# Eleven of the thirteen gate products that stand behind the RWKV chain move into seven earlier lumps

## What is computed

```python
def token_mixer(h, ...):
    p = h @ w_in
    p_r, p_m, p_g = jnp.split(p, [RWKV_COLS, RWKV_COLS + MLSTM_COLS], axis=-1)
    y_r = rwkv7_branch(p_r, ...) @ branch_w_rwkv
    y_m = mlstm_branch(p_m, ...) @ branch_w_mlstm
    g_r, g_m = jnp.split(jax.nn.sigmoid(p_g.astype(jnp.float32)), 2, axis=-1)
    return ((g_r * y_r + g_m * y_m) @ w_out).astype(h.dtype)
```

## Time and profile before

| what | value |
|---|---|
| median of 3 runs | 1408.33 us (1407.04 to 1410.0) |
| the profiled execution's own time | 1409.51 us |
| its span in the profile | 1407.5 us |
| PE busy | 1385.3 us, 98% of the span |
| granted PE clock, mean | 0.999 |
| share of PE in the chain that ended last | 96% |
| instructions on PE and PEld | 2 x 13536 |
| instruction packets on queue q8 | 106, 1.74 MB |

### The profile page before, as it was taken

One profiled execution on the slowest core, in us unless ns is written; L12 is line 12 of the kernel. 1 busy time (PEld: TensorE's weight loads), 2 busy tenths in 40 slices (PEclk: granted clock), 3 DMA queues, 4 the chain that ended last, 5 costly groups with the idle time before them and its releaser, 6 DMA issues.

```text
span 1407.5 us, 30467 instructions
## 1 busy us (share of the span) xinstructions
PE 1385.3 (98%) x13536; PEld 1304.2 (93%) x13536; DVE 1028.7 (73%) x1718; ACT 288.4 (20%) x556; POOL 67.6 (5%) x137
## 2 busy tenths in 40 slices
PE   7999999999999999999999999999999999999998
PEld 3999999888978999999999999988998889999998
DVE  5899889778524769897988886787873375856565
ACT  2211101452222031110031110034332302211101
POOL 5000000000000000100000000000000000000000
PEclk9999999999999999999999999999999999999999
DMA  9999785443423658888767886554433257456530
GB/s 347 325 328 326 284 316 172 141 141 106 113 71 122 236 183 269 278 303 291 246 211 254 275 280 237 167 133 151 140 90 96 65 192 251 144 188 209 195 136 30
DMA packets 214051, 283.10 MB, mean 201 GB/s; under 512 B 13289, under 2 KB 177505, under 8 KB 213921
## 3 DMA queue, kind: packets, MB, share of 16 engines
q1 hardware_dynamic: 194976, 211.11, 46.5%
q0 software_dynamic: 17952, 69.21, 14.0%
q10 hardware_dynamic: 992, 0.85, 0.2%
HBM read 280.10 MB, written 1.05 MB: 200 GB/s over the span
## 4 chain that ended last, share of the span: by engine, by line
PE 96%; DVE 2%; DMA 1%; issue 1%; ACT 0%; ACTq 0%; SPq 0%; DVEq 0%
PE ps L1833 94%; PE ps L1837 1%; DVE ada_acc L1045 1%; DMA ada_stage<-in_ada_w_dram 1%; DMA xn<-in_x_dram 0%; PE ps L2332 0%; DVE ada_turn L1051 0%; DVE ada_red L1052 0%; DVE arena L1274 0%; DVE arena L1277 0%; DVE arena L1275 0%; DVE hT L1818 0%; ACT xn L696 0%; ACT hT L696 0%; DVE x L1218 0%
## 5 line engine op out<-in xcount | busy, mean ns | idle before, releaser
L1833 PE MATMUL ps<-hT,ring 128*128 128x128 f32 (+2 forms) x2448 | 394.3, 318 | 3.4 <-issue 2.1
L1833 PEld LDWEIGHTS ps<-hT,ring 128*128 128x128 f32 (+1 forms) x2448 | 349.9, 190 | 37.7 <-issue 10.7
L1833 PE MATMUL ps<-y_both,arena 128*128 128x128 f32 x2304 | 266.6, 275 | 1.0 <-issue 1.0
L1833 PEld LDWEIGHTS ps<-y_both,arena 128*128 128x128 f32 x2304 | 261.8, 192 | 1.5 <-issue 1.5
L1833 PE MATMUL ps<-arena 32*32 32x32 f32 (+6 forms) x4368 | 203.1, 230 | 2.5 <-issue 2.4
L1833 PEld LDWEIGHTS ps<-arena 32*32 32x32 f32 (+3 forms) x4368 | 192.6, 138 | 11.9 <-issue 9.8
L1833 PE MATMUL ps<-arena,ring 128*128 128x128 f32 (+1 forms) x1312 | 186.5, 294 | 0.0
L1833 PEld LDWEIGHTS ps<-arena,ring 128*128 128x128 f32 x1312 | 171.3, 191 | 6.6
L1045 DVE SCALAR_TENSOR_TENSOR ada_acc<-ada_stage,cond,ada_acc 128x1024 f32<-128x1024 f32 (+1 forms) x119 | 149.0, 1252 | 5.6 <-DMA ada_stage<-in_ada_w_dram 1.6
L1833 PE MATMUL ps<-y_both,ring 128*128 128x128 f32 (+1 forms) x1024 | 150.8, 301 | 0.0
L1833 PEld LDWEIGHTS ps<-y_both,ring 128*128 128x128 f32 x1024 | 138.7, 192 | 6.5
(11 more groups left out here) (317 smaller groups left out, 1341.4 us busy)
## 6 DMA issues: line engine op xcount, KB each, us to landing
ring<-in_ffn_w_in_dram SPq DMA_DIRECT2D x86, 1024.0 KB, 7.7
ada_stage<-in_ada_w_dram POOLq DMA_DIRECT2D x66, 1024.0 KB, 5.7
ring<-in_ffn_w_out_dram SPq DMA_DIRECT2D x44, 1024.0 KB, 6.7
ring<-in_mix_w_in_dram SPq DMA_DIRECT2D x46, 512.0 KB, 5.2
ring<-in_mix_w_in_dram SPq DMA_DIRECT2D x12, 1024.0 KB, 5.7
ring<-in_mix_w_in_dram SPq DMA_DIRECT2D x6, 1536.0 KB, 6.4
ring<-in_mix_w_out_dram SPq DMA_DIRECT2D x8, 1024.0 KB, 5.0
arena<-in_ada_w_dram SPq DMA_DIRECT2D x6, 1024.0 KB, 13.6
```

Source lines behind the costliest of these rows:

```text
L1833: return nc.tensor.matmul(out_, lhsT, rhs, start=start, stop=stop, **kw)
```

## The change

Only the table of places changes. The sum of all places stays 96, the products keep their numbers, and so their order, their weights and their banks.

```diff
-GATE_PLACES = (("num", 5), ("n", 8), ("a", 8), ("b", 8), ("c", 8), ("d", 8), ("e", 8), ("f", 9), ("h", 7),
-               ("i", 4), ("j", 5), ("k", 5), ("tail", 13))
+GATE_PLACES = (("num", 5), ("n", 10), ("a", 10), ("b", 10), ("c", 9), ("d", 9), ("e", 10), ("f", 10), ("h", 7),
+               ("i", 4), ("j", 5), ("k", 5), ("tail", 2))
```

## The result

The changed kernel takes 1416.78 us (median of 6 runs, 1411.51 to 1419.99) against 1409.06 us of the kernel before on the same chip (6 runs, 1407.04 to 1410.07): 7.7 us or 0.5% slower, ratio 1.0049 with a 95% interval of 1.0032 to 1.0066. I had forecast 1408.8 us and a range that ended at 1412.0 us. Only the direction, slower, came as forecast; the size and the range were wrong. The 1416.8 us lies beyond even the slower rival (B).

A forecast was written before the change was run, and what follows sets the result against it. The prediction took PE's work plus the holes in it, late instruction packets, as the bound. Its terms, 0 + 0 + 0 + 0.5 us on a median of 1408.33 us, gave 1408.8 us, range 1404.4 to 1412.0 us.

The forecast's parts named there:

- rival (B): Tile 7's start in lump `i` puts the `branch_w_mlstm` transfer over 64x64-run packets in both layers: +4.1 us, 1412.4 us; chance 0.16.
- What bounds the kernel: Whole span: PE's work plus its holes, 6.1 us in both stretches, which are waits for the next instruction packet.
- the recipe for the size of the holes: Boundaries every 128 pairs; a packet needs 3.0 us quiet, 4.8 us inside a weight transfer, against PE's time on 128 pairs.
- Products that move: Eleven tail products, 4.75 us a layer, go into the lumps at the same size, bank and clock: net 0.
- What the lumps cover: In the lumps: no hole is ended by DVE or ACT, so longer lumps cover what is covered already: 0.
- What the tail covered: Behind the shorter tail: cover used up but not gone, some 0.9 us to spare at the transposes: 0.
- Rival (C): The tail's cover fails, `r normed` later than PE at the transposes: 1410.5 to 1411 us; chance 0.04.
- Instruction packets: Holes in both stretches: 4.4 us in layer 0 and 3.0 us in layer 1, recipe against recipe +0.5 us.
- The clock has nothing to give back.: Both stretches: PE's granted clock is already 1.00, the level of 2.4 GHz, so no gain was counted from it.
- The page's rule: Crossing a 256-instruction block is "mostly hidden"; by it the packet term would be 0 and the time 1408.3 us.

The follow-up runs named there:

- e2: The changed kernel with 36 small matmuls (72 pairs) more at PE's start, so all packet boundaries fall 72 pairs earlier: 1410.35 us.
- e3: The kernel before with 24 small matmuls (48 pairs) more at PE's start: 1413.93 us.
- e8: The kernel before with 46 small matmuls (92 pairs) more at PE's start, ahead of the wait for x: 1405.69 us.
- e7: The changed kernel with the SP wait of e1 and 76 pairs of small matmuls more at PE's start, ahead of the wait for x: 1401.80 us.
- e1: The changed kernel with SP waiting for 'chain 2' ahead of each layer's second `branch_w_mlstm` transfer, which also holds the `branch_w_rwkv` one behind it: 1408.56 us.
- e9: The changed kernel with SP holding back only each layer's first `branch_w_rwkv` transfer until 'chain 2': 1413.15 us.
- e11: e7 with the change undone: the places of before, SP's wait and the 76 pairs kept: 1404.26 us.
- e6: The kernel before with one forced hole a layer: PE waits for DVE's "r centred" ahead of the tail products: 1418.16 us.
- e4: The kernel before with the eleven tail products put into lump `h` alone, `n` to `f` as they were: 1415.57 us.

## Why the prediction was wrong

**What bounds the kernel** stood: PE's work and the holes in it, and the holes are instruction packets. e2, e3 and e8 move nothing but the boundaries, and so does e7 against e1; e1 and e9 move nothing but transfers. All shift the time by holes and clock, in the direction that this reading gives, though the recipe for the size of the holes missed in e3 and e11.

**Products that move, 0.** Right: no row of a gate product at full clock has another price per record, and e1 has the time of the kernel before.

**What the lumps cover, 0.** Right in that no hole is ended by DVE or ACT in either kernel.

**What the tail covered, 0.** Right, 0.93 us to spare where 0.9 was forecast. Rival (C) didn't come.

**Instruction packets, +0.5 us.** This step failed, in size: in the profiled execution the holes grew by 4.6 us (10.72 against 6.12 us). Layer 0 came as laid out: holes of 0.4, 1.4 and 2.5 us were forecast and 0.52, 1.69 and 2.17 us measured, at those places, and those of 1.13 and 1.34 us went. Layer 1 was forecast with 3.0 us and had 6.34 us. Of the 3.3 us missed, 2.1 us is the hole at the end of the run of 160 pairs, 3.56 us in place of 1.5. I had followed the `branch_w_mlstm` transfer through SP's queue and not the one queued behind it, which was then free to leave on its own at DVE's `qt`; e9 shows that one at work. Another 1.7 us is the hole ahead of lump `b`, 2.06 us in place of 0.4. Its packet met a transfer that SP had issued at 1069.23 us and started only as that burst ended, 13.3 us into the stretch. In e1 and e9, with the same order up to there, it started 12.9 and 12.3 us into the stretch, in e9 with q1 still at 115%, and the holes had 1.47 and 1.05 us: where in a burst the packet gets through varies between executions. That this packet meets a transfer at all may come from tile 3's start, two products earlier in `a`; no run tests that apart. Also wrong was to take 4.8 us as the most that a packet needs in traffic: from its boundary to 1134.95 us this one took nearly 6 us (2.43 us of records and 3.56 us of hole).

**"The clock has nothing to give back."** This sentence failed outright: it put the clock at 0 because it could not rise. But it could fall, and the forecast of a 2.5 us hole should have carried that price. The stretches of the kernel before have no hole that long, but its end has the sign: PE's last product is done at 1402.67 us, and the granted clock is 0.50 from about 1404.0 us on. Three falls of some 1.65 us are 5 us of the profiled execution's 10.5 us, as much as the holes. That execution is the slowest of the six, and over all of them the share is smaller: the mean granted clock of the six runs is 0.996, that of the 23 runs of the kernel before beside e1 0.9977. Over a span of 1418 us the difference is 2.4 us of the 7.7 us, an estimate, as each run's clock is given to 0.001 only. With the holes as I forecast them and one fall behind the 2.5 us, the term would have been +2.2 us and the time 1410.5 us; with the second transfer seen, a second fall and 2.1 us more, 1414.2 us.

**The rival (B)** had the mechanism and the place and was too cheap, for the same two reasons. It held "just not in layer 1, where lump `j` lies between", which is true of the first transfer only.

**The page's rule** (Trainium skill, "Runtime: NRT & Kernel Launch", section on instruction fetch mechanics), that the crossing of a block is mostly hidden: the runs agree in one place and not in another. Between the two stretches, 606.13 us with 4775 pairs and so some 37 crossings, all idle time of PE is 0.66 us. In the stretches the changed kernel pays 10.7 us of holes, and e7, with the same dense runs, none: there it depends on where the crossings fall and what transfers they meet.

What stays open: 1 us of e6, the 0.35 us in layer 0, why some holes of about 2 us are followed by a fall and others not, and how often exactly the timed runs have one. The changed kernel's runs spread over 8.5 us, and the profile shows only the slowest. The fastest, 1411.51 us, is the one with a mean granted clock of 0.999; the other five have 0.993 to 0.997. So it probably had no fall, and the 2.4 us that it still lost are holes.

## What to carry to other kernels

On an engine that runs many short instructions, lay the boundaries of its instruction packets over the program and look which weight transfer goes out at each: an edit that moves the release of a buffer moves that transfer and every one queued behind it, and a transfer over a dense stretch can stop the engine that it was meant to feed. Price a hole on PE not by its length alone: in these runs holes of 1.93 (e9), 2.06, 2.13, 2.17, 2.26, 2.27 and 3.56 us were followed by 3.4 us or more at half clock, while others of 1.95 (e1), 2.09 (e6) and 2.20 us (e4) were not. A kernel that differs by a few matmuls at its start is not the same kernel to the instruction queue, so a change of this size is judged only after the alignment has been varied too.

## What the runs showed of the hardware that I had not expected

The changed kernel took 1416.8 us, and 1401.8 us with 76 small pairs ahead of it and one wait on SP: 1% by the alignment and the time of two transfers, with every product kept. A packet of instructions can be held up by a weight transfer in progress: at all three long holes of the changed kernel it starts as q1 runs dry, while in the kernel before (386.1 us) and in e9 (1072.5 us) one got through with q1 at 107 and 115%. What decides this no run shows. And 38 small matmuls in four groups of rows took 1.28 us, inside PE's idle 2.4 us ahead of x, where 36 in one group took 4.01 us.
